# Halves of rows for groups 3 to 6 of the scan inputs and groups 3 and 4 of the up projections

## The reference

```python
def first_block(x, ...):
    for layer in range(2):
        h = rmsnorm(x, attn_norm_g[layer])
        proj = h @ w_in[layer]                  # 1024 x 8208
        gm_u, gm_v, ssm_z, ssm_xbc, ssm_dt, da_q, da_k, da_v, gates = split_cols(proj, IN_SIZES)
        ...
        y_b = mamba2_mixer(ssm_z, ssm_xbc, ssm_dt, ...)
        ...
        h = rmsnorm(x, ffn_norm_g[layer])
        up = causal_dwconv(h @ ffn_w_up[layer], ffn_conv_w[layer], ffn_conv_b[layer])
        gate, val = jnp.split(up, 2, axis=-1)   # 2816 each
        x = x + (jax.nn.silu(gate) * val) @ ffn_w_down[layer]

def mamba2_mixer(z, xbc, dt_raw, ...):
    xbc = jax.nn.silu(causal_dwconv(xbc, conv_w, conv_b))   # 1536 channels, 4 taps
    dt = jax.nn.softplus(dt_raw + dt_bias)
    y = ssd_scan(...)                                       # takes xbc and dt
    return rmsnorm(y * jax.nn.silu(z), norm_g)

def second_block(h, ...):
    for layer in range(2):
        h = h + _token_mixer(_rmsnorm(h, norm1[layer]), ...)
        h = h + _conv_ffn(_rmsnorm(h, norm2[layer]), ...)   # gelu(conv(a)) * gval, then w_down
    return _rmsnorm(h, norm_f)
```

## Time and profile before

| | us |
|---|---|
| median of 3 runs | 1810.81 |
| lowest and highest | 1810.40, 1810.84 |
| the profiled execution | 1810.84 |
| its span in the trace | 1808.8 |

### The profile page before, as it was taken

How to read it: one execution, slowest core, us unless ns; L and a number is a source line. 1 busy time by engine, 2 the same in 40 slices (tenths; PEclk the granted TensorE clock), 3 DMA queues, 4 the chain that set the end, 5 groups by cost and what they waited for, 6 DMA issues and landing times.

```text
span 1808.8 us, 26088 instructions
## 1 busy us (share of the span) xinstructions
PE 1796.9 (99%) x10250; PEld 1571.0 (87%) x10250; DVE 1383.1 (76%) x2040; ACT 1045.8 (58%) x1287; POOL 19.8 (1%) x45
## 2 busy tenths in 40 slices
PE   8999999999999999999999999999999999999998
PEld 8898889888989888898889888898889888889887
DVE  6968887997697887799868756679957765578974
ACT  6667646775565774577645456555544456556543
POOL 2000000000000000000000000000000000000000
PEclk9999999999999999999999999999999999999999
DMA  9986556655988665555556565555556565555553
GB/s 223 209 164 155 174 184 189 202 192 184 181 165 162 162 177 177 172 186 187 196 180 194 178 191 184 180 169 192 191 179 196 180 195 187 175 179 185 192 181 105
DMA packets 254961, 328.01 MB, mean 181 GB/s; under 512 B 25908, under 2 KB 169536, under 8 KB 254840
## 3 DMA queue, kind: packets, MB, share of 16 engines
q1 hardware_dynamic: 254576, 326.00, 61.9%
q10 hardware_dynamic: 264, 0.35, 0.1%
HBM read 325.23 MB, written 1.09 MB: 180 GB/s over the span
## 4 chain that ended last, share of the span: by engine, by line
PE 97%; DMA 1%; SPq 1%; ACT 0%; DVE 0%; issue 0%; DVEq 0%; ACTq 0%
PE psum L717 19%; PE psum L656 16%; PE psum L658 16%; PE psum L657 16%; PE psum L728 10%; PE psum L644 10%; PE psum L763 5%; DMA w_raw<-in_w_in 1%; PE psum L865 1%; PE psum L947 0%; PE psum L1099 0%; PE psum L1079 0%; PE psum L667 0%; PE psum L1086 0%; PE psum L1077 0%; PE psum L988 0%
## 5 line engine op out<-in xcount | busy, mean ns | idle before, releaser
L424 ACT ACTIVATE w_hi<-w_raw 128x2048 fp32r<-128x2048 f32 (+2 forms) x309 | 574.1, 1859 | 283.0 <-PE psum L658 247.2
L412 DVE TENSOR_TENSOR w_low<-w_raw,w_hi 128x1024 fp32r<-128x1024 f32 (+1 forms) x310 | 373.9, 1206 | 233.1 <-ACT w_hi L424 225.9
L656 PE MATMUL psum<-w_hi,act 128*128 128x512 f32 x1248 | 492.1, 394 | 0.0
L658 PE MATMUL psum<-w_hi,act 128*128 128x512 f32 x1248 | 486.4, 390 | 0.0
L657 PE MATMUL psum<-w_low,act 128*128 128x512 f32 x1248 | 486.0, 389 | 0.0
L416 DVE TENSOR_TENSOR w_low<-w_raw,w_hi 128x1024 fp32r<-128x1024 f32 (+2 forms) x307 | 360.6, 1175 | 0.0
L717 PE MATMUL psum<-act,w_hi 128*128 128x512 f32 x1536 | 360.3, 390 | 0.0
L717 PEld LDWEIGHTS psum<-act,w_hi 128*128 128x128 f32 x1536 | 284.3, 188 | 56.4
L658 PEld LDWEIGHTS psum<-w_hi,act 128*128 128x128 f32 x1248 | 234.3, 188 | 49.3
L656 PEld LDWEIGHTS psum<-w_hi,act 128*128 128x128 f32 x1248 | 234.5, 188 | 47.0 <-DVE w_low L416 0.3
L657 PEld LDWEIGHTS psum<-w_low,act 128*128 128x128 f32 x1248 | 234.6, 188 | 46.5
(11 more groups left out here) (285 smaller groups left out, 1573.7 us busy)
## 6 DMA issues: line engine op xcount, KB each, us to landing
w_raw<-in_w_in SPq DMA_DIRECT2D x121, 1024.0 KB, 6.0
w_raw<-in_ffn_w_up SPq DMA_DIRECT2D x40, 1024.0 KB, 5.1
w_raw<-in_w_up SPq DMA_DIRECT2D x40, 1024.0 KB, 5.1
w_raw<-in_ffn_w_down SPq DMA_DIRECT2D x16, 1024.0 KB, 5.2
w_raw<-in_w_down SPq DMA_DIRECT2D x16, 1024.0 KB, 5.0
w_raw<-in_w_branch_b SPq DMA_DIRECT2D x8, 1024.0 KB, 5.0
w_raw<-in_w_out SPq DMA_DIRECT2D x8, 1024.0 KB, 5.1
w_raw<-in_w_a SPq DMA_DIRECT2D x8, 1024.0 KB, 5.4
```

The costliest lines, as they stand in the source:

```text
L412: dve.tensor_tensor(lo[:, 0:cut, :], of[:, 0:cut, :], hi[:, 0:cut, :], ALU.subtract).then_inc(w_lo_front, 1)
L424: act.activation(group_view(whi, q % HIGH, g), group_view(raw, q % LOW, g), ACT.Copy).then_inc(w_hi, 1)
L656: mm(o, xh, hi[:, k, :], start=g["opens"] and k == 0, stop=False)
L658: last = mm(o, xl, hi[:, k, :], start=False, stop=g["closes"] > 0 and k == g["kt"] - 1)
```

## The change

Four things change.

- **Loads.** `ROW_HALVES` says how many groups at the start of a kind are halves of the rows: six of XBC (before: two), two of PU as before, four of UP (before: two). So `XBC2`/`XBC3`, `XBC4`/`XBC5` and `UP2`/`UP3` become pairs, each half with 512 columns. The loads of `XBC2` to `XBC5` have lines of 2 KB in place of 1 KB. `UP2` and `UP3` come as two DMAs each, and their lines stay at 1 KB. All groups stay at 1 MB.
- **TensorE.** `high_first` runs a pair, two row tiles at a time over both banks; `later_pair` runs the others. The count and shapes of matmuls stay. In `pair_products` the wait on x's parts is now one for each two row tiles, and `first_pair` no longer waits for a whole half ahead of its first matmul.
- **ScalarE and VectorE.** The names in `LATER` (`XBC2`, `XBC4`, `UP2`) behave as those in `FIRST`: the split of the group three places later stands ahead of the take, and the take waits on `first_bank`, which now comes after three quarters of the pair in place of the end of the pair's first group.
- A condition on PU in block 1 goes; block 1 has no PU group.

```diff
+    ROW_HALVES = dict(XBC=6, PU=2, UP=4)
...
-                if g["kind"] in ("XBC", "PU", "UP") and g["n"] < 2:
-                    g.update(kt=4, cols=512, k0=4 * g["n"])
+                if g["n"] < ROW_HALVES.get(g["kind"], 0):
+                    g.update(kt=4, cols=512, k0=4 * (g["n"] % 2))
...
+    LATER = ("XBC2", "XBC4", "UP2")
+    OPENERS = FIRST + LATER
...
-            def pair_products(b, i, n, G, half, bank_at, a0):
+            def pair_products(b, i, n, G, half, bank_at, a0, ready=None, done=0):
                 for t in range(2):
                     for k in range(4):
+                        if ready is not None and (bank_at, t) == (0, 0) and k % 2 == 0:
+                            pe.wait_ge(step(ready), done + 2 * half + (k // 2 + 1))
                         if (bank_at, t, k) == (0, 0, FRONT[4]):
                             pe.wait_ge(w_lo_back, q + 1)
...
+            def later_pair(b, i, n, G, half):
+
+                third = G[n]["name"] in ("XBC2", "UP2")
+                ready = "h_ready" if third else None
+                done = norm_count(b, i, G[n]["kind"] == "UP", 0)
+                if half:
+                    pe.wait_ge(w_lo_front, plain_count(b, i, n + 2))
+                    pair_products(b, i, n, G, 1, 0, G[n]["tile"], ready, done).then_inc(step("first_bank"), 1)
+                else:
+                    proj_waits(b, i, n, G)
+                    pair_products(b, i, n, G, 0, 0, G[n]["tile"], ready, done)
+                    bank_wait(b, i, n + 1, G[n + 1]["bank"])
+                pair_products(b, i, n, G, half, 1, G[n]["tile"]).then_inc(group_done, 1)
...
                 if (b, i, n) == (1, 0, 0):
                     return first_pass_pair(G, turn_rest, spread_rest, a0)
-                pe.wait_ge(step(ready), before + 2)
                 proj_waits(b, i, n, G)
-                pair_products(b, i, n, G, 0, 0, a0)
+                pair_products(b, i, n, G, 0, 0, a0, ready, before)
...
-                pe.wait_ge(step(ready), before + 4)
                 pe.wait_ge(w_lo_front, plain_count(b, i, n + 2))
-                pair_products(b, i, n, G, 1, 0, a0).then_inc(step("first_bank"), 1)
+                pair_products(b, i, n, G, 1, 0, a0, ready, before).then_inc(step("first_bank"), 1)
...
-                    if g["name"] in FIRST:
+                    if g["name"] in OPENERS:
                         split_behind(1, i, n)
                     take(n, g)
...
-                    if g["name"] not in FIRST and g["name"] != "DN0":
+                    if g["name"] not in OPENERS and g["name"] != "DN0":
                         split_behind(1, i, n)
...
             def arrived(b, i, n):
                 g = PASS[b, i][n]
-                if g["name"] in FIRST:
+                if g["name"] in OPENERS:
                     dve.wait_ge(step("first_bank"), pair_count(b, i, g))
```

More of the change, by code:

```diff
@@ L309, in loaded_count @@
         def loaded_count(q):
-            return 16 * sum(2 if GROUPS[p][3]["kind"] == "UP" and GROUPS[p][3]["n"] < 2 else 1 for p in range(q % LOW, q + 1, LOW))
+            return 16 * sum(2 if GROUPS[p][3]["kind"] == "UP" and GROUPS[p][3]["n"] < ROW_HALVES["UP"] else 1 for p in range(q % LOW, q + 1, LOW))
         def pair_count(b, i, g):
-            return (0 if b == 1 else 2 * LAYERS) + 2 * i + (g["kind"] == "UP") + 1
+            q = at_group(b, i, at_name[b][g["name"]])
+            return sum(GROUPS[p][3]["name"] in OPENERS for p in range(q + 1))
         def closing(i, g):
@@ L814, in high_first @@
                         dt_products(0)
-                    for ks in (range(0, 4), range(4, 8)):
+                    for ks in (range(0, 2), range(2, 4)):
                         if low:
@@ L1030, in stream @@
                     first_pair(b, i, n, G, *firsts[G[n]["name"]])
-                elif n == 0 or G[n - 1]["name"] not in firsts:
-                    third = G[n]["name"] in ("XBC2", "Q0", "UP2")
+                elif G[n]["name"] in LATER or n and G[n - 1]["name"] in LATER:
+                    half = G[n]["n"] % 2
                     if (b, i, G[n]["name"]) == (1, 0, "XBC2"):
@@ L1035, in stream @@
                     if (b, i, G[n]["kind"]) == (1, 0, "XBC"):
-                        return high_first(n, G)
+                        return high_first(n - half, G, half)
+                    later_pair(b, i, n - half, G, half)
+                elif n == 0 or G[n - 1]["name"] not in firsts:
+                    third = G[n]["name"] in ("XBC2", "Q0", "UP2")
                     proj(b, i, n, G, norm_count(b, i, G[n]["kind"] == "UP", 0) if third else None)
@@ L2332, in _ @@
                         b2_max(SC_AT[g["name"]])
[L2333 removed]
+                    if g["name"] not in OPENERS and MERGED.get(g["name"]) != 0:
                         split_behind(2, i, n)
```

70 lines of the change are left out of this document (37 added, 33 removed).

## The result

The changed kernel takes 1814.68 us (median of 14 runs) against 1810.60 for the kernel before (14 runs beside them). The ratio is 1.0021, with an interval of 1.0013 to 1.0029: 4.1 us or 0.2% slower, where 1812.0 was forecast. That is in the direction of the forecast and beyond it by more than twice the forecast's 1.2. The profiled execution took 1814.2, and its span is 1812.1. One of the 14 runs, at a clock of 0.75, took 2218 us: the ratio leaves it out, and without it the median is 1814.62.

What follows compares the result with a forecast made beforehand. TensorE, 97% of the chain that ended last, was taken as the bound; 1810.84 + 0.4 + 0.9 - 0.9 + 0.8 gave 1812.0 us, with a range from 1809.0 to 1814.5.

Steps and rivals of the forecast that it cites:

- term 4: UP2 in block 2: its taps end later, TensorE waits on UP7's low part, 0.4 in each of two layers, +0.8.
- term 1: XBC2 to XBC5 in layer 0: gap ahead of XBC4 closes, dt_proj starts 0.7 later, later waits give 0.3, net +0.4.
- L + 7.3: Layer 0: the dt sum is ready 7.3 us after XBC5 lands at L = 39.0, so at 46.3.
- rival C: Layer 0's loads come early, so dt_proj goes by TensorE alone, -1.5 there; 1809.0 in all, chance 0.11.
- Rival D: Layer 0: XBC5 lands late and TensorE stands at dt_proj for the dt sum; 1816.1 at 125 GB/s, chance 0.06.
- The argument from line length: Loads of XBC4 and XBC5: 2 KB lines taken at 165 GB/s, 6.4 us each, against 112 for 1 KB in layer 0.
- Rival B: The longer lines bring nothing: XBC5 lands as before, the dt sum is ready at 48.0; 1813.7, chance 0.15.
- Term 2: Layer 1: XBC5's low part on VectorE moves ahead of the taps and dt sum, so TensorE waits at dt_proj, +0.9.
- Term 3: Waits on x pair by pair: two UP0 of block 1 (0.33 each) and PU0 (0.25) gain, -0.9.
- the missing six waits: Sign: the six waits of 0.2 on parts of x, at UP0 four times, XBC0 and PU0 in layer 1, are gone.
- the wait at UP7: Sign: TensorE waits about 0.9 on the low part of UP7 in block 2, twice.
- The stop of about 2.2: Sign: TensorE stops ahead of layer 0's dt_proj (46.3 against 44.15) until the dt sum ends the stop.

Runs made afterwards that it cites:

- Experiment 4: The changed kernel with nine extra matmuls of 128x512 filling the stop ahead of layer 0's dt projection: 1813.44 us.
- Experiment 5: The changed kernel with the back of XBC5's low part in layer 0 on VectorE instead of GpSimd: 1812.83 us.
- experiment 10: The changed kernel with the old order on ScalarE and VectorE, and XBC3 to XBC5 each loaded as two 256-column DMAs with 1 KB lines: 1809.28 us.
- Experiments 2 and 3: The changed kernel with the old order on both ScalarE and VectorE, 1809.03 us; and with the old order on VectorE alone, 1810.36 us.
- Experiment 8: The kernel before, with only the waits on the parts of x in the first pairs made two row tiles at a time: 1810.32 us.
- Experiment 9: The changed kernel with the old order on ScalarE and VectorE and the old waits on x in the first pairs: 1810.26 us.

## Why the prediction was right or wrong

**Direction and range.** The forecast was a loss of 1.2, too small to be told from no change. The measured loss is 4.1 us, 0.22%, and clear of noise. The median lies just past the border of 0.2% from which the forecast said slower, with a chance of 0.07, but the interval of the ratio, 0.13% to 0.29%, lies across that border, so which of the two cases it is can't be told. The time of 1814.68 is 0.2 above the range's end of 1814.5, and the interval, 1813.2 to 1816.1 from 1810.84, lies across that end too. Of the rivals none is the case: what happened is the forecast's mechanisms, term 4's twice as dear, and in term 1 a price that it left out.

**Term 1, +0.4, measured +1.5.** The gap closed (-1.5 for -1.45), the dt projection started at 46.44 for a forecast 46.3, and the waits behind gave 0.35 back for 0.3. The step that failed is the one that ends with the stop itself: 2.15 us of TensorE standing still were priced at 2.15. The stop cost 1.9, and behind it the clock fell to its lower level and cost 1.5 more. Experiment 4 shows that it was the stop. The trace of the kernel before could not have given this price: its longest stop in this stretch is 1.29, and behind the one of 1.80 that ends at 10.43 the clock stays at 1.00.

That 46.3 was hit is luck. The step took XBC5's landing, L = 39.0, as what sets the dt sum, L + 7.3. In fact L was 35.4 (XBC3 landed 1.4 sooner than taken, and the two loads took 5.7 and 4.9 for the 6.4 each), and the sum stood behind VectorE's own work: taps of XBC1 up to 38.1, then two fronts, XBC4's beside XBC5's, of which GpSimd held one up by 1.7. By L = 35.4 the same sum gives 42.7. The landing was put 3.6 too late, and the second front and the collision were missed; they came to the same. (The addends as the text gives them, 1.92, 1.2, 2.96 and 1.4, come to 7.5 and not to 7.3, which changes none of this.) Experiment 5 shows the collision. With the loads that early, rival C's condition was met, and its result (-1.5) didn't come, as it also took the load for the bound. Rival D had the place right, and priced it by a load that was never late.

The argument from line length was wrong for the gap. The rows of 112 and 145 GB/s were of different columns, which the text said, and it took them as a price of the line all the same. The Trainium skill, "DMA: Bandwidth & Descriptors", Specifications, asks for at least 512 B per transfer for line rate, which lines of 1 KB meet. In experiment 10 the trace agrees as far as this gap goes; both loads together still took 12.1 us with 1 KB lines and 9.8 with 2 KB. Rival B, by which nothing would come sooner, was wrong too: the halves themselves close the gap.

**Term 2, +0.9, measured +0.9.** As forecast. The dt projection waits 0.76 where it had waited for nothing, with the low part, the taps and the sum in a row ahead of it. Experiments 2 and 3 take it away by the order on VectorE. One detail is off: the 0.45 that TensorE gains in XBC0 to XBC3 is not lost in this wait but ahead of it, at XBC4, where a low part is 0.4 late (L768 on L420 in the waits above), and experiments 2 and 3 lose it there too.

**Term 3, -0.9, measured -1.05.** The size is right, the reason only half. I held the third group's wait for a small extra. Experiment 8 shows it as a condition: without halves in the third group the 0.3 is lost again at once. Experiment 9 shows that the halves alone don't win it. (The 48 matmuls of the earlier trace rows are one half of the rows over both banks; the description of `first_pair` ahead of the prediction counts them for each bank, which is twice too many.)

**Term 4, +0.8, measured +1.6.** The place and the mechanism are right, the size is half. The back of UP7's low part was 4.3 later in the trace, and of these 2.0 are the lateness with which TensorE came to UP0: a shift of 2.3 for the forecast 2.0, and the slack was 1.5 for 1.6. VectorE's two waits for ScalarE are in the rows, 1.26 and 1.11, together 2.4; I had counted the low part's 2.3 and then taken 0.3 off for ScalarE's copy behind. A difference of two numbers of about 2 is not known to 0.3 when each is known to 0.3.

**The first 25 us**, +0.5 in the profiled pair, were in no term. They differ from execution to execution: the start of XBC2 lay between 24.7 and 26.0 in the profiles of all kernels here, and in some the clock fell there too. In experiment 8's profile, which was 0.9 us late at 18 us:

```profile
10.00:14.00 4.00, 3.88 (x23) 3.91 (x24) 2.91 (x4) 1.31 (x2) 0.00 (x0) 0.68 1.07 250
```

That stretch follows a stop of 2.04 us. So a difference of half a microsecond between two single profiles can be the start alone.

**What would show it**: the stops at both dt projections, the missing six waits, and the wait at UP7 were all there. The stop of about 2.2 was 1.92 of idle time, 2.2 from the start of the last matmul ahead of it (44.24) to 46.44. That the copies start at 34 and 39 was not so: 31.6 and 35.7.

## What to carry to other kernels

Price a stop of the bound engine with what may come behind it: here a stop that cost 1.9 us by itself cost 3.4 with the slow stretch behind it. When work is moved ahead of a small result that the bound engine needs (a dt sum of 0.8 us), count the slack of that result and not of the work; the same halves with the old order turned a loss of 4.1 us into a gain of about 1.5. And where VectorE and GpSimd work at the same time, look at the other's rows before taking an instruction's length from elsewhere.
